# The final norm moved into the last item's branches of an expert loop, on one core

## Chip, cores and metric

One NeuronCore of a Trainium2 chip runs the whole kernel. The metric is the device time in microseconds (us), the median of several runs.

## What is computed

One decoder block on 1024 tokens of width 1024, in fp32: a mixer (short convolution, differential attention, attention into a memory), a feed-forward part in which each token goes to 4 of 32 experts, and a final RMSNorm. The change concerns the last two steps:

```python
x = x + moe_ffn(h, router_w[l], router_b[l], w_gate_up[l], b_gate_up[l], w_down[l], b_down[l])
return rmsnorm(x, final_norm_g)      # y = x * rsqrt(mean(x * x) + eps) * g
```

`moe_ffn` gives each token the sum of its four experts' outputs, each times its gate.

## The kernel before

**Phases.** The mixer and the router run first (about 590 us). They leave in HBM the rows of x (`residual_rows`, `acc_d` in the code), the normed rows for the experts (`h_d`), and for each expert the list of its tokens.

**Items.** The rest is a loop over items. An item is one expert with up to 256 of its rows: one block of 128 rows, a full one and a short one of 64, or two full ones. A table computed on the chip holds each item's expert, list and size. Every engine runs the same loop (groups of 4, inside it `it`) and reads the sizes of this and the next item from the table. `by_size` picks one of three bodies written out one behind the other: `("full",)`, `("full", "short")`, `("full", "full")`. There are 35 items; the last has one block.

**An item's work.** The expert's weights come in 12 units of 1 MB (units 0 to 7 gate and up, 8 to 11 down), each into its slot of `weight_ring`; `home(u)` is the slot of unit u. Each matmul is done in parts: ACT copies a unit to a high half (`high_unit`, L1150), VectorE subtracts for the low half, in place in the ring (`low_unit`, L1564), and TensorE uses both (`use_unit`, L688). It counts `w_used` up per unit, after which SyncE may load the slot anew. Between the units ACT computes the sigmoid of the gate (L1185, L1191), VectorE the product (L1603 to L1622), and TensorE turns the result (L922), which ACT and VectorE split (`a_high` L1198, `a_low` L1585) before the down units. The order on each engine is written out by hand in `item`: on ACT `high_unit` 8 and 9, the next item's x (`x_high`), `high_unit` 10 and 11, `a_high` 1, next item's units, `results`; on VectorE `low_unit` 9, `x_low` 0 of the next item (L1575), `low_unit` 10, `a_low` 1, `low_unit` 11, and so on. Units 10 and 11 on TensorE need `a_low` 1.

**Rows in and out.** GpSimd gathers the rows of an item two items ahead (L603) and adds the results, which ACT writes to `y_rows` (L1211), to `residual_rows` by a scatter that adds (L609). For a missing second block it makes an empty transfer (L651, L660), which is there to move a counter.

**The end.** When the last item's scatter has landed, GpSimd signals `all_added`. SyncE then loads the 8 tiles of 128 rows from `residual_rows` into slots of the ring (L532) and the gain of the final norm, one row spread over 128 partitions (L534, its second transfer). Per tile ACT squares and sums (L1276) and takes the root (L1278), for which it loads another function table than the sigmoid's; VectorE takes the reciprocal (L1690) and multiplies (L1691); SyncE writes the tile out (L537).

Of the kernel before, what the change touches and what calls it, by code (L numbers as in the profile page):

```python
# [67 lines left out]
SHORT = P // 2  # L68
LIST = EXPERTS * S
# [17 lines left out]
def hymba_kernel(nc, a, out):  # L87
    ctx = ExitStack()
    with ctx:
        def sb(name, shape, dt=f32):  # L90
            return ctx.enter_context(nc.sbuf_tensor(name, shape, dt))
# [32 lines left out]

        def final_tile(t):

            return ring[:, t // 2, D * (t % 2):D * (t % 2) + D]
# [70 lines left out]
        def w_low_part(u):  # L198
# [50 lines left out]
        e_rstd = sb("e_rstd", [P, NT])  # L249
        h2T = wk[:, 5, :].rearrange("p (k t) -> p k t", k=KD)  # L250
# [41 lines left out]
            "gain_in", "idx_in", "idx_moved", "idx_kept", "all_added", "pick_made",  # L292
# [13 lines left out]
        s_fout = sem("final_out")  # L306
        s_gf = sem("final_gain_in")
# [104 lines left out]
        def _(sp):  # L412
# [117 lines left out]
            sp.wait_ge(s["all_added"], 1)  # L530
            for t in range(NT):
                sp.dma_start(final_tile(t), acc_d[P * t:P * t + P, :]).then_inc(s_final[t], 16)  # L532
                if t == 0:
                    sp.dma_start(wk[:, 5, :], a["final_norm_g"].partition_broadcast(P)).then_inc(s_gf, 16)  # L534
# [7 lines left out]
        def _(pool):  # L542
# [69 lines left out]

            load_list(slice(0, CAP))
# [20 lines left out]
            with pool.Fori(0, MAX_ITEMS // GROUP) as group:  # L634
                size_group = pool.value_load(table[2:3, bass.ds(group * GROUP + 1, 1)], min_val=0, max_val=CAP + 1)
                with pool.If(size_group > 0):
                    with pool.Fori(0, GROUP) as place_in:
# [4 lines left out]
                        with pool.If(size_now > 0):  # L642
                            with pool.If(size_far > 0):
# [10 lines left out]
                            pool.wait_ge(s["y_made"], it * 2 + 3)  # L654
                            pool.sem_inc(s["pool_waited"], 1)
                            scatter(0)
                            pool.wait_ge(s_scatter[0], it * 16 + 32)
                            pool.sem_inc(s["pool_waited"], 1)
                            by_second(pool, size_now, lambda kind: scatter(1, kind),
                                      lambda: pool.dma_start(nothing[0:1, 1, :], ident[0:1, 0:16]).then_inc(s_scatter[1], 16))  # L660
                            pool.wait_ge(s_scatter[1], it * 16 + 32)
                            pool.sem_inc(s["pool_waited"], 1)
                            with pool.If(size_next > 0):
                                pool.wait_ge(s["idx_kept"], it + 1)
# [15 lines left out]
                            with pool.Else():  # L680
                                pool.sem_inc(s["all_added"], 1)
# [327 lines left out]
        def _(act):  # L1009
# [205 lines left out]

            def item(it, size_next, kinds):
# [56 lines left out]

            for t in range(NT):
                act.wait_ge(s_final[t], 16)
                act.activation(wk[:, 4, :], final_tile(t), ACT.Square, accum_out=e_ssq[:, t:t + 1]).then_inc(s["act_chain"], 1)  # L1276
                act.wait_ge(s["act_chain"], 18 + t + 1)
                act.activation(e_std[:, t:t + 1], e_ssq[:, t:t + 1], ACT.Sqrt, scale=1.0 / D, bias=eps[:, :]).then_inc(s_fsq, 1)  # L1278
# [3 lines left out]
        def _(dve):  # L1282
# [350 lines left out]

            def item(it, size_next, kinds):
# [52 lines left out]
            dve.wait_ge(s_gf, 16)  # L1687
            for t in range(NT):
                dve.wait_ge(s_fsq, t + 1)
                link(dve.reciprocal(e_rstd[:, t:t + 1], e_std[:, t:t + 1]))  # L1690
                dve.scalar_tensor_tensor(out=final_tile(t), in0=final_tile(t), scalar=e_rstd[:, t:t + 1], in1=wk[:, 5, :],  # L1691
                                         op0=ALU.mult, op1=ALU.mult).then_inc(s_fdone, 1)

# [22 lines left out]
```

## Time and profile before

| | us |
|---|---|
| median of 3 runs (lowest, highest) | 2270.81 (2268.62, 2271.24) |
| the profiled execution, reported time | 2271.15 |
| the profiled execution, its span | 2269.5 |
| TensorE busy, share of the span | 2156.5, 95% |
| VectorE busy | 1557.7, 69% |
| ACT busy | 1331.5, 59% |
| GpSimd busy | 340.2, 15% |

The span is from the first to the last event of the execution; the reported time has 1.65 us around it. A share of busy time is a mean over stages with different limits, so a stage is read by itself, with the timelines of its engines side by side. ACT is the scalar engine, DVE VectorE, POOL GpSimd, SP SyncE.

### The profile page before, as it was taken

What the parts mean: (1) busy time and instruction counts of PE and PEld (TensorE: products, weight loads), DVE (VectorE), ACT (ScalarE), POOL (GpSimd) and SP (SyncE); (2) the same over time, 40 slices, a digit from 0 to 9 for tenths busy, and PEclk for the clock granted to TensorE, in tenths of its full rate; (3) what the DMA queues carried; (4) which work ended last, traced back from release to release, by engine and by line L of the source; (5) the groups of instructions that cost most, each with busy time, mean ns of one, the idle gap of its engine ahead of it and who ended that gap; (6) DMA issues with size and microseconds to landing.
All of it is one profiled execution on the core that took longest, in us unless ns stands there. A gap on an engine that the chain in (4) does not pass through costs nothing.

```text
span 2269.5 us, 34559 instructions
## 1 busy us (share of the span) xinstructions
PE 2156.5 (95%) x10770; PEld 1790.6 (79%) x10771; DVE 1557.7 (69%) x1641; ACT 1331.5 (59%) x1524; POOL 340.2 (15%) x306
## 2 busy tenths in 40 slices
PE   7999999895999999999999999999999999999993
PEld 6889767895778888877887878788888878888882
DVE  4411289566577577589758989886677897767764
ACT  5111179443565466577657777775555777556654
POOL 1000000023111022022112121221210122111200
PEclk9999989997999999999999999999999999999997
DMA  5111300434787689599869999996676999677854
GB/s 198 57 56 38 111 1 1 183 106 132 260 292 237 207 294 344 192 365 376 306 206 372 371 368 359 371 343 232 222 234 226 355 373 333 228 232 240 306 162 171
DMA packets 265277, 536.75 MB, mean 237 GB/s; under 512 B 14478, under 2 KB 31144, under 8 KB 265132
## 3 DMA queue, kind: packets, MB, share of 16 engines
q1 hardware_dynamic: 248332, 488.26, 60.3%
q0 software_dynamic: 16896, 47.83, 8.6%
q8 instruction: 32, 0.52, 0.1%
q14 instruction: 17, 0.14, 0.0%
HBM read 499.29 MB, written 36.75 MB: 236 GB/s over the span
## 4 chain that ended last, share of the span: by engine, by line
PE 83%; issue 6%; DVE 5%; ACT 3%; DMA 1%; POOL 0%; DVEq 0%; SPq 0%; ACTq 0%; POOLq 0%
PE ps L688 79%; PE ps L915 1%; ACT hT_hi L1150 1%; PE ps L922 1%; DVE hT_lo L1575 1%; DVE w_lo L1564 1%; PE ps L825 1%; ACT region_mem L1185 0%; DVE work L1615 0%; DVE hT_lo L1585 0%; DMA weight_ring<-in_w_mix_in 0%; ACT hT_lo L1198 0%; DVE weight_ring L1691 0%; DVE work L1393 0%; DVE m_max L1355 0%
## 5 line engine op out<-in xcount | busy, mean ns | idle before, releaser
L688 PE MATMUL ps<-hT_hi,hT_lo 128*128 128x512 f32 (+1 forms) x4304 | 1396.4, 388 | 13.2 <-DVE hT_lo L1585 12.3
L688 PEld LDWEIGHTS ps<-hT_hi,hT_lo 128*128 128x128 f32 x4304 | 806.7, 188 | 182.4 <-DVE w_lo L1564 18.2
L1150 ACT ACTIVATE hT_hi<-weight_ring 128x2048 fp32r<-128x2048 f32 x417 | 786.1, 1914 | 174.8 <-PE ps L688 118.4
L1564 DVE TENSOR_TENSOR slots_between<-weight_ring,hT_hi 128x2048 fp32r<-128x2048 f32 x245 | 552.5, 2286 | 129.5 <-ACT hT_hi L1150 128.9
L688 PE MATMUL ps<-slots_between,hT_lo 128*128 128x512 f32 x1344 | 525.7, 391 | 0.0
L1564 DVE TENSOR_TENSOR w_lo<-weight_ring,hT_hi 128x2048 fp32r<-128x2048 f32 x140 | 319.8, 2285 | 33.6 <-ACT hT_hi L1150 33.6
L688 PE MATMUL ps<-w_lo,hT_lo 128*128 128x512 f32 (+1 forms) x896 | 336.0, 375 | 0.0
L688 PEld LDWEIGHTS ps<-slots_between,hT_lo 128*128 128x128 f32 x1344 | 253.4, 189 | 53.9
L688 PEld LDWEIGHTS ps<-w_lo,hT_lo 128*128 128x128 f32 x896 | 168.7, 188 | 30.3
L609 POOL DMA_INDIRECT residual_rows<-work,idx_now x48 | 121.8, 2537 | 469.5 <-ACT work L1211 274.9
L603 POOL DMA_INDIRECT work<-normed_rows,idx_far x49 | 86.2, 1759 | 442.1 <-PE ps L915 269.8
L688 PE MATMUL ps<-mem_there,picked 128*128 128x512 f32 x288 | 123.5, 429 | 8.8 <-issue 5.9
L1585 DVE TENSOR_TENSOR hT_lo<-ps,hT_lo 128x512 fp32r<-128x512 f32 x96 | 58.9, 636 | 99.1 <-ACT hT_lo L1198 99.1
L1185 ACT ACTIVATE region_mem<-ps,limits 128x512 f32<-128x512 f32 x78 | 52.3, 681 | 123.1 <-PE ps L688 122.6
L688 PE MATMUL ps<-hT_hi,w_hi 128*128 128x512 f32 x256 | 101.1, 395 | 7.5 <-DVE hT_lo L1309 7.5
L589 POOL DMA_INDIRECT expert_lists<-pay,dest_i x32 | 32.6, 1020 | 497.2 <-DVE dest_i L1494 489.9
L1592 DVE TENSOR_TENSOR work<-ps,work 64x512 f32<-64x512 f32 x54 | 36.8, 682 | 101.1 <-ACT work L1169 54.4
L688 PE MATMUL ps<-hT_lo,w_hi 128*128 128x512 f32 x256 | 100.4, 392 | 0.0
L688 PE MATMUL ps<-hT_hi,w_lo 128*128 128x512 f32 x256 | 100.4, 392 | 0.0
L1334 DVE COPY weight_ring<-ps 128x512 f32<-128x512 f32 x18 | 12.4, 691 | 124.5 <-PE ps L688 124.5
L1160 ACT ACTIVATE hT_lo<-ps 128x512 fp32r<-128x512 f32 (+1 forms) x96 | 48.3, 556 | 69.2 <-PE ps L915 69.2
L688 PE MATMUL ps<-last_slot,hT_lo 128*128 128x512 f32 (+1 forms) x256 | 87.2, 364 | 0.0
(251 smaller groups left out, 2418.6 us busy)
## 6 DMA issues: line engine op xcount, KB each, us to landing
weight_ring<-in_w_gate_up SPq DMA_DIRECT2D x280, 1024.0 KB, 7.8
weight_ring<-in_w_down SPq DMA_DIRECT2D x140, 1024.0 KB, 6.3
weight_ring<-in_w_mix_in SPq DMA_DIRECT2D x10, 1024.0 KB, 5.8
weight_ring<-in_x SPq DMA_DIRECT2D x8, 512.0 KB, 8.1
weight_ring<-in_w_mix_out SPq DMA_DIRECT2D x4, 1024.0 KB, 5.3
work<-in_x SPq DMA_DIRECT2D x8, 512.0 KB, 4.6
residual_rows<-work SPq DMA_DIRECT2D x8, 512.0 KB, 3.3
normed_rows<-work SPq DMA_DIRECT2D x8, 512.0 KB, 3.6
```

The lines of the kernel that those rows point to most:

```text
L589: pool.indirect_dma_start(list_d[:, :], bass.IndirectOffsetOnAxis(ap=dest_i[:, i, c:c + 1], axis=0), pay[:, i, c, :], None).then_inc(s["li ...
L603: pool.indirect_dma_start(xg[rows, b, :], None, h_d[:, :], bass.IndirectOffsetOnAxis(ap=idx_far.bitcast(i32)[rows, b, 0:1], axis=0)).then_ ...
L609: pool.indirect_dma_start(acc_d[:, :], bass.IndirectOffsetOnAxis(ap=idx_now.bitcast(i32)[rows, b, 0:1], axis=0), y_rows[rows, b, :], None, ...
L688: return pe.matmul(o, l, r, start=first, stop=last)
L825: last = pe.transpose(ps[:, 4 + b // 4, P * (b % 4):P * (b % 4) + P], wk[:, 2 * (n % 2), P * b:P * b + P], ident[:, :])
L915: last = pe.transpose(ps[:, bank + half, P * k:P * k + P], xg[:, b, HALF * half + P * k:HALF * half + P * k + P], ident[:, :])
L1150: act.activation(w_high_part(u), ring[:, home(u), :], ACT.Copy).then_inc(s["w_high_made"], 1)
L1160: ins = act.activation(x_split[:, 4 * half:4 * half + 4, b, 0, cols], ps[:, bank + half, :].rearrange("p (k t) -> p k t", t=P)[:, :, cols] ...
L1185: ins = act.activation(sig_b[rows, b, :], gate_b[rows, b, :] if kind == "short" else ps[:, out_bank("g", c, b, kinds), :], ACT.Relu, scale ...
L1564: dve.tensor_tensor(w_low_part(u), ring[:, home(u), :], w_high_part(u).bitcast(f32), ALU.subtract)\
L1585: ins = dve.tensor_tensor(low_place(a_split[:, ks, b], kind), ps[:, turn_bank(c, b), :].rearrange("p (k t) -> p k t", t=P)[:, :, cols], a_ ...
L1592: dve.tensor_tensor(place, ps[0:SHORT, bank, :], place, ALU.add).then_inc(s["sum_made"], 1)
```

## The change

The stage behind the loops is gone. Its work goes into the branches that an engine takes in the last item (`size_next` is 0):

- GpSimd, on entering the last item, signals `earlier_added`. It gathers the item's own rows of `residual_rows` into SBUF, and at the end, when these rows are finished (`rows_made`) and all 8 tiles are written out (`s_fout`), scatters them into `out`, without adding. The adding scatter and the empty transfer of the last item are gone.
- SyncE, in the last item, waits for `earlier_added`, loads the 8 tiles into the slots of units 0 to 3 as these are used, and behind them the gain into the slot of unit 4. Its loop checks the size of this item rather than the next, so that it gets there.
- ACT: `final_squares` for tiles 0 to 3 where `x_high` 0 of the next item would stand, for tiles 4 to 7 where the next item's units would stand; each waits for the gain first, takes one root over four tiles and ends with a load of the sigmoid's table. Behind `results` it squares the item's own rows (`rows_std_of`).
- VectorE: `final_norms` for four tiles at the answering places, and `rows_finished` for the item's own rows.

The diff, cut to its core (a line "..." marks what is left out):

```diff
         def final_tile(t):
 
-            return ring[:, t // 2, D * (t % 2):D * (t % 2) + D]
+            return ring[:, home(t // 2), D * (t % 2):D * (t % 2) + D]
...
 (SyncE)
-                size_group = sp.value_load(table[2:3, bass.ds(group * GROUP + 2, 1)], min_val=0, max_val=CAP + 1)
+                size_group = sp.value_load(table[2:3, bass.ds(group * GROUP + 1, 1)], min_val=0, max_val=CAP + 1)
...
+                        with sp.Else():
+                            now = sp.value_load(table[2:3, bass.ds(k + 1, 1)], min_val=0, max_val=CAP + 1)
+                            with sp.If(now > 0):
+                                sp.wait_ge(s["earlier_added"], 1)
+                                for t in range(NT):
+                                    sp.wait_ge(s["w_used"], k * 12 + (HI_SLOTS + t // 2 + 1))
+                                    sp.dma_start(final_tile(t), acc_d[P * t:P * t + P, :]).then_inc(s_final[t], 16)
+                                sp.wait_ge(s["w_used"], k * 12 + (HI_SLOTS + FINAL_GAIN_UNIT + 1))
+                                sp.dma_start(final_gain(), a["final_norm_g"].partition_broadcast(P)).then_inc(s_gf, 16)
...
 (GpSimd, last item)
-                                pool.sem_inc(s["all_added"], 1)
+                                pool.sem_inc(s["earlier_added"], 1)
+                                for b in range(BLOCKS):
+                                    pool.wait_ge(s_xturned[b], it + 1)
+                                pool.sem_inc(s["pool_waited"], 1)
+                                rows_gather(0)
...
+                                pool.wait_ge(s["rows_made"], 1)
+                                pool.wait_ge(s_fout, 16 * NT)
+                                pool.sem_inc(s["pool_waited"], 1)
+                                rows_scatter(0)
...
 (ACT)
+            def final_squares(n, tiles):
+                act.wait_ge(s_gf, 16)
+                for t in tiles:
+                    act.wait_ge(s_final[t], 16)
+                    act.wait_ge(s["act_chain"], 18 + t)
+                    act.activation(final_junk(), final_tile(t), ACT.Square, accum_out=e_ssq[:, t:t + 1]).then_inc(s["act_chain"], 1)
+                act.wait_ge(s["act_chain"], 18 + tiles[-1] + 1)
+                cols = slice(tiles[0], tiles[-1] + 1)
+                act.activation(e_std[:, cols], e_ssq[:, cols], ACT.Sqrt, scale=1.0 / D, bias=eps[:, :]).then_inc(s_fsq, 1)
+                act.preload_act_table(ACT.Sigmoid)
+
+            def rows_std_of(kinds):
+                act.preload_act_table(ACT.Sqrt)
+                act.wait_ge(s["act_chain"], 18 + NT)
+                for b, kind in enumerate(kinds):
+                    act.wait_ge(s["rows_summed"], b + 1)
...
+                act.preload_act_table(ACT.Sigmoid)
...
                 with act.If(size_next > 0):
                     x_high(0, it + 1, "full")
+                with act.Else():
+                    final_squares(0, FINAL_EARLY)
                 high_unit(it, 10)
                 high_unit(it, 11)
                 a_high(it, 1, kinds)
...
+                with act.Else():
+                    final_squares(1, FINAL_LATE)
                 for c in range(2):
                     results(it, c, kinds)
...
+                with act.If(size_next < 1):
+                    rows_std_of(kinds)
...
 (VectorE)
+            def final_norms(n, tiles):
+                dve.wait_ge(s_fsq, n + 1)
+                cols = slice(tiles[0], tiles[-1] + 1)
+                dve.reciprocal(e_rstd[:, cols], e_std[:, cols]).then_inc(s["final_rstd"], 1)
+                dve.wait_ge(s["final_rstd"], n + 1)
+                for t in tiles:
+                    dve.scalar_tensor_tensor(out=final_tile(t), in0=final_tile(t), scalar=e_rstd[:, t:t + 1], in1=final_gain(),
+                                             op0=ALU.mult, op1=ALU.mult).then_inc(s_fdone, 1)
+
+            def rows_finished(it, kinds):
+                dve.wait_ge(s["y_made"], it * 2 + 3)
...
                 with dve.Else():
                     dve.sem_inc(s_xlow[0], 1)
+                    final_norms(0, FINAL_EARLY)
                 low_unit(it, 10)
                 a_low(it, 1, kinds)
...
+                with dve.If(size_next < 1):
+                    final_norms(1, FINAL_LATE)
+                    rows_finished(it, kinds)
```

## Rows read from the trace of the kernel before

**Rows 1.** Waits: engine, line, waited for: us in total, times, longest.

```profile
POOL nothing L660 <- DMA residual_rows<-work,idx_now: 162.8, 22, 8.7
```

**Rows 2.** Windows, one-block item: PE, PEld, DVE, ACT, POOL busy, PEclk, DMA share, GB/s.

```profile
1254.50:1291.70 37.20, 36.39 (x168) 29.71 (x167) 32.85 (x23) 28.31 (x23) 7.67 (x8) 1.00 1.05 375
```

**Rows 3.** Timeline, same item, VectorE and TensorE: start, us, [idle before <-releaser].

```profile
1280.72 2.29 DVE L1564 TENSOR_TENSOR w_lo<-weight_ring,hT_hi 128x2048 fp32r<-128x2048 f32 x1
...
1283.75 0.47 PE L688 MATMUL ps<-hT_hi,hT_lo 128*128 128x512 f32 x1 [0.81 <-DVE hT_lo L1585]
```

**Rows 4.** Chain of waits that ended last, the tail: start, us, what.

```profile
2235.84 6.12 DMA residual_rows<-work,idx_now
...
2242.75 1.56 DMA nothing<-ident
...
2244.62 0.36 SPq L532
...
2245.49 6.10 DMA weight_ring<-residual_rows
...
2251.62 1.16 ACT work L1276 x2
```

**Rows 5.** Timeline, last item and tail, ACT.

```profile
2217.21 7.32 ACT L1150 ACTIVATE hT_hi<-weight_ring 128x2048 fp32r<-128x2048 f32 x4
...
2234.36 0.69 ACT L1211 ACTIVATE work<-ps,idx_now 128x512 f32<-128x512 f32 x1 [1.89 <-PE ps L688]
2247.86 1.06 ACT L1276 ACTIVATE work<-weight_ring 128x1024 f32<-128x1024 f32 x1 [12.81 <-DMA weight_ring<-residual_rows]
...
2249.02 1.28 ACT L1278 ACT_TABLE_LOAD   x1
2250.32 0.30 ACT L1278 ACTIVATE e_std<-e_ssq,eps 128x1 f32<-128x1 f32 x1
```

**Rows 6.** Timeline, the items before the last, GpSimd.

```profile
2142.07 0.76 POOL L598 DMA_DIRECT2D idx_far<-expert_lists  x1 [1.36 <-issue]
...
2215.32 0.19 POOL L666 COPY idx_now<-idx_next 128x4 f32<-128x4 f32 x1 [5.00 <-DMA residual_rows<-work,idx_now]
```

**Rows 7.** Timeline, TensorE: after an idle stretch early on; unit 9 of the last item.

```profile
418.93 1.12 PE L849 MATMUL ps<-ident,region_v 128*128 128x128 f32 x4 [4.60 <-DVE region_v L1433]
...
2225.62 0.50 PE L688 MATMUL ps<-mem_there,picked 128*128 128x512 f32 x1 [0.45 <-DVE w_lo L1564]
```

**Rows 8.** SyncE's timeline; DMA issues 2235 to 2270: count, KB, us to landing.

```profile
2245.49 4.08 SPq L532 DMA_DIRECT2D weight_ring<-residual_rows  x7
...
out_rows<-weight_ring SPq DMA_DIRECT2D x8, 512.0 KB, 6.7
work<-in_final_norm_g SPq DMA_DIRECT2D x1, 512.0 KB, 5.3
```

**Rows 9.** Windows in the tail, columns as in rows 2.

```profile
2247.50:2248.50 1.00, 0.00 (x0) 0.00 (x0) 0.00 (x0) 0.64 (x1) 0.00 (x0) 0.50 0.67 242
...
2251.50:2252.50 1.00, 0.00 (x0) 0.00 (x0) 0.71 (x1) 0.88 (x1) 0.00 (x0) 0.50 1.02 418
```

**Rows 10.** Timeline, tail, VectorE.

```profile
2253.33 1.28 DVE L1691 SCALAR_TENSOR_TENSOR weight_ring<-weight_ring,e_rstd,work 128x1024 f32<-128x1024 f32 x1
```

**Rows 11.** Windows around idle stretches of TensorE, for the granted clock (PEclk).

```profile
423.00:424.00 1.00, 1.00 (x10) 1.00 (x9) 1.00 (x5) 0.00 (x0) 0.00 (x0) 0.86 1.05 387
...
2238.00:2240.00 2.00, 0.00 (x0) 0.00 (x0) 0.00 (x0) 0.00 (x0) 0.00 (x0) 0.79 0.90 125
```

**Rows 12.** All gathers of L603: from issue to landing.

```profile
DMA to landing us min/median/max: 4.1/7.1/9.1
```

**Rows 13.** Timeline, ACT at the start of two one-block items.

```profile
1254.53 5.53 ACT L1150 ACTIVATE hT_hi<-weight_ring 128x2048 fp32r<-128x2048 f32 x3 [1.56 <-issue]
...
2200.24 5.62 ACT L1150 ACTIVATE hT_hi<-weight_ring 128x2048 fp32r<-128x2048 f32 x3 [0.72 <-issue]
```

**Rows 14.** DMA queues between 400 and 650 us: packets, MB, share.

```profile
q8 instruction: 15, 0.25, 0.4%
```

More of the change, by code:

```diff
@@ L68 @@
 SHORT = P // 2
+FINAL_GAIN_UNIT = 4
+FINAL_EARLY, FINAL_LATE = range(0, 4), range(4, S // P)
 LIST = EXPERTS * S
@@ L306, in hymba_kernel @@
         s_fout = sem("final_out")
+        s_rows_in = [sem(f"rows_in{b}") for b in range(BLOCKS)]
+        s_rows_out = [sem(f"rows_out{b}") for b in range(BLOCKS)]
         s_gf = sem("final_gain_in")
@@ L611, in scatter, with rows_gather, rows_scatter @@
                     y_rows[rows, b, :], None, compute_op=ALU.add).then_inc(s_scatter[b], 16)
+            def rows_gather(b, kind="full"):
+                rows = rows_of(kind)
+                pool.indirect_dma_start(
+                    xg[rows, b, :], None, acc_d[:, :],
+                    bass.IndirectOffsetOnAxis(ap=idx_now.bitcast(i32)[rows, b, 0:1], axis=0)).then_inc(s_rows_in[b], 16)
+            def rows_scatter(b, kind="full"):
+                rows = rows_of(kind)
+                pool.indirect_dma_start(
+                    out[0, :, :], bass.IndirectOffsetOnAxis(ap=idx_now.bitcast(i32)[rows, b, 0:1], axis=0),
+                    y_rows[rows, b, :], None, bounds_check=S - 1, oob_is_err=False).then_inc(s_rows_out[b], 16)
             load_list(slice(0, CAP))
@@ L652, in _ @@
                                 pool.sem_inc(s["pool_waited"], 1)
[L654 to L662, printed above, removed]
-                            with pool.If(size_next > 0):
+                            with pool.If(size_next > 0):
+                                pool.wait_ge(s["y_made"], it * 2 + 3)
+                                pool.sem_inc(s["pool_waited"], 1)
+                                scatter(0)
+                                pool.wait_ge(s_scatter[0], it * 16 + 32)
+                                pool.sem_inc(s["pool_waited"], 1)
+                                by_second(pool, size_now, lambda kind: scatter(1, kind),
+                                          lambda: pool.dma_start(nothing[0:1, 1, :], ident[0:1, 0:16]).then_inc(s_scatter[1], 16))
+                                pool.wait_ge(s_scatter[1], it * 16 + 32)
+                                pool.sem_inc(s["pool_waited"], 1)
                                 pool.wait_ge(s["idx_kept"], it + 1)
@@ L1214, in results @@
                 ins.then_inc(s["rest_made"] if "short" in kinds else s["y_made"], 1)
+            def final_squares(n, tiles):
[13 more added lines that the diff above has]
+                    act.wait_ge(s["rows_summed"], b + 1)
+                    rows = rows_of(kind)
+                    act.activation(final_junk()[rows, :], xg[rows, b, :], ACT.Square, accum_out=rows_ssq[rows, b:b + 1])\
+                        .then_inc(s["rows_squared"], 1)
+                    act.wait_ge(s["rows_squared"], b + 1)
+                    act.activation(rows_std[rows, b:b + 1], rows_ssq[rows, b:b + 1], ACT.Sqrt, scale=1.0 / D, bias=eps[rows, :])\
+                        .then_inc(s["rows_std"], 1)
+                act.preload_act_table(ACT.Sigmoid)
             def item(it, size_next, kinds):
@@ L1272, in _ @@
                             act.sem_inc(s["act_item"], 1)
[L1274 to L1278, printed above, removed]
         @block.vector
@@ L1632, in results @@
                     dve.tensor_scalar(place, place, idx_now[0:SHORT, b, 1:2], None, ALU.mult).then_inc(s["y_made"], 1)
+            def final_norms(n, tiles):
[8 more added lines that the diff above has]
+                dve.wait_ge(s["y_made"], it * 2 + 3)
+                for b, kind in enumerate(kinds):
+                    rows = rows_of(kind)
+                    dve.wait_ge(s_rows_in[b], 16)
+                    dve.tensor_tensor(xg[rows, b, :], y_rows[rows, b, :], xg[rows, b, :], ALU.add).then_inc(s["rows_summed"], 1)
+                for b, kind in enumerate(kinds):
+                    rows = rows_of(kind)
+                    dve.wait_ge(s["rows_std"], b + 1)
+                    dve.wait_ge(s["rows_summed"], b + 1)
+                    dve.reciprocal(rows_rstd[rows, b:b + 1], rows_std[rows, b:b + 1]).then_inc(s["rows_rstd"], 1)
+                    dve.wait_ge(s["rows_rstd"], b + 1)
+                    ins = dve.scalar_tensor_tensor(out=y_rows[rows, b, :], in0=xg[rows, b, :], scalar=rows_rstd[rows, b:b + 1],
+                                                   in1=final_gain()[rows, :], op0=ALU.mult, op1=ALU.mult)
+                ins.then_inc(s["rows_made"], 1)
             def item(it, size_next, kinds):
@@ L1685, in _ @@
                             dve.sem_inc(s["dve_item"], 1)
[L1687 to L1692, printed above, removed]
 _INS = ["x", "mem", "rel_bias", "attn_norm_g", "w_mix_in", "conv_w", "lambda_qk", "diff_subln_g", "mem_norm_g",
```

22 lines of the change are left out of this document (16 added, 6 removed).

## Prediction

> **What bounds the kernel now.** The page's first part, busy time by engine, names TensorE, and the loop over the items is its loop. Most items have one block of 128 rows: 22 of 35 make the empty transfer that stands for a missing second block [rows 1]. In such an item, 37.20 us long, TensorE works 36.39 us [rows 2] and loses 0.81 us once, waiting for the split of the activations on VectorE [rows 3]. The change leaves TensorE's program alone, so what it can win is in the tail; the chain of waits and the timelines of the last 40 us are the views to read, engine by engine.
>
> The tail of now: the last result leaves ACT at 2235.05 (2234.36 + 0.69) [rows 5]. GpSimd starts the adding scatter at 2235.84 and it lands 6.12 us later; an empty transfer takes 1.56 us more; the first tile is asked for at 2244.62 and the last write ends the span at 2269.5 [rows 4]. That is 34.5 us behind the last result. The DMA engines are the limit of its second half: 8 tiles in, the gain, 8 tiles out, 8.9 MB at about 420 GB/s, with a slow stretch at 242 GB/s where the gain is broadcast [rows 9]. The change wants to do the 8 tiles while TensorE still works, and leave only the last item's own rows for the end.
>
> **The change part by part.** The sum follows the last item in the clock of the profiled execution (span 2269.5, reported 2271.15, so 1.65 around it; the median of the three runs is 2270.81, 0.34 below the profiled one).
>
> *When the loads can start.* GpSimd says that the earlier items are added when it enters the last item. Its last act in the item before is the copy that ends at 2215.51 [rows 6]. Then it waits for its own signal and reads the table three times. Elsewhere such a wait, one read and the making of a transfer cost 1.36 us of idle time together [rows 6]. So three reads cost between 0.5 and 3.2 us; I take 2.3, and the first tile is asked for at 2217.8. The slots are long free by then: TensorE is past units 0 to 4, which are used in order ahead of unit 9, and that one begins at 2225.62 [rows 7].
>
> *When the gain lands.* SyncE asks for 8 tiles, 0.58 us each [rows 8], and for the gain last. The queue delivers in the order asked: now the first tile lands 3.24 us after its request (2244.62 to 2247.86) [rows 4, 5], the gain, asked second, takes 5.3 us [rows 8], and ACT gets the second tile, asked for at 2245.49, 6.10 us later [rows 4]. In the changed kernel 4.19 MB of tiles and GpSimd's gather of the last item's rows (0.52 MB) go ahead of it. These 4.71 MB take 11.2 us at 420 GB/s, the gain 2.2 us at 242 GB/s [rows 9], and 2.0 us go to start and completion (the first tile's 3.24 less the 1.2 that its 0.52 MB take): 15.4 us, so the gain is there at 2233.2.
>
> *What waits for it.* This is the heart of it. The first act of `final_squares` is a wait for the gain, and on ACT this stands ahead of `high_unit` 10, 11 and `a_high` 1. Without the gain ACT would get there at 2220.9, two of its four weight copies after 2217.21 [rows 5]; it now stands until 2233.2, and TensorE's units 10 and 11 wait behind it. TensorE is done with unit 9 at about 2228.5 and then idles for 19 us.
>
> *ACT from 2233.2:* four squares with their sums, 1.16 each [rows 4] and a signal between, 4.9; table load 1.28; root 0.30 [rows 5]; signal to VectorE at 2239.7. Table of the gate, 1.28: 2241.0. Weight copies 10 and 11, 1.83 each (7.32 / 4), and `a_high`, 0.6: 2245.3. Then the late four tiles: squares to 2250.2, load and root to 2251.8, table of the gate to 2253.1.
>
> *VectorE from 2239.7:* reciprocal and four products at 1.28 (1.2 apart) [rows 10]: 2244.8. The low half of weight 10 at 2.29 (2.2 apart) [rows 3]: 2247.1; the split of the activations, 0.69: 2247.7; low half 11: 2249.9.
>
> *TensorE:* unit 10 begins at 2247.85. When it stopped at 2234.3 in the kernel before, its clock was down to half in the stretch 2238 to 2240 (granted 0.79 of full) and it came back only 4.3 us after work began at 418.93 (0.86 in 423 to 424) [rows 7, 11]. So I charge the first 4.4 us at half clock: 10 matmuls at 0.45 us, the other 14 of the two units at 0.23 (36.39 us for 168 of them, transposes among them, are 0.22 each [rows 2]): 2255.6. ACT's second result is done at 2256.3, which is 21 us later than now.
>
> *The tail behind that:* VectorE finishes the late four products (from 2251.9) at 2256.9 and adds the gathered rows (1.2): 2258.2. Square and sum on ACT 1.25, root 0.30, reciprocal 0.2, product 1.28: 2261.4. From ACT's result to the start of a scatter GpSimd took 0.79 us [rows 4, 5]: 2262.2. A scatter without adding isn't in the trace: gathers of the same size land in 4.1 us at best [rows 12], the adding scatter of the undisturbed tail in 6.12 [rows 4]; I take 5.0, nearer to the quiet gather, whose traffic is the same: 2267.2. The eighth tile's write, asked for at 2257.0, lands in at most 6.7 us [rows 8], 2263.7, so its wait comes at worst 1.5 us later than the rows are ready, and at best is hidden. GpSimd then goes through the loop once more, three reads: 1.5 us. End at 2268.9.
>
> So the sum is 0.6 us under the span of now: 34.5 us of tail become 12.6, and 21 of the 22 us are paid back as a hole in the middle of the last item. As a reported time 2270.5 for the profiled execution, 2270.2 for the median.
>
> *What every item pays.* ACT skips two new blocks and one at the end, VectorE one longer block and one at the end. ACT's gap between items is 0.72 us where it falls through to the end of the loop body, and 1.56 where it jumps over the two other bodies [rows 13], so a jump costs between 0 and 0.84. ACT has cover, for it is busy 28.31 of an item's 37.20 us [rows 2] and waits for TensorE in the rest. VectorE's next low half follows with no idle time where a jump stands today [rows 3]. I take nothing. If the cover is gone, the delay adds to TensorE's 0.81.
>
> A rule that speaks against the change is on the Trainium skill's page "Runtime: NRT & Kernel Launch", section "Instruction fetch mechanics": a taken branch to code outside a small window forces a fetch by DMA and stalls. In this trace the queues of instructions carry packets up to 650 us [rows 14] and have no row between 660 and 2200 us, where the loop runs more than 30 times; so today the bodies fit. No run shown has the longer ones.
>
> The page "ScalarE: Activation LUTs" of the Trainium skill, section "What ACT_TABLE_LOAD costs", adds a drain of about 1.38 us to every switch. The trace disagrees: the square begins at 2247.86, the load 1.16 us later, which is what a square with its sum takes [rows 4], and the root begins 0.02 us after the load's end [rows 5]. By the page's figure the three switches on the path would make the sum 4.1 us longer.
>
> **The rivals.** *The gain comes early.* If its packets don't queue behind the tiles, it lands 5.3 us after its request at 2222.4, at 2227.7, 5.5 us earlier, and all behind it moves along: 2264.7. For it: the transfers use 16 engines, and order between them isn't proven. Against: the landings of now come in the order asked.
>
> *The jumps are uncovered.* In each of 22 items VectorE's jump over the longer block, between the split of x and the low half of weight 10, delays the split of the activations for which TensorE already waits [rows 3]. At 0.84 each that is 18 us: 2288. It decides from 0.2 us an item. For it: there is no slack behind. Against: a jump stands there already and shows nothing.
>
> *The loop outgrows its instruction buffer.* ACT's three bodies grow by half. Each item would then fetch code on ACT; the price of a small transfer is at least the 1.56 us of the empty one [rows 4], twice an item, once to leave a body and once to come back: 3.1 us in each of 34 items, 106 us with nothing covered, half of it if ACT's idle time takes the other half: 2323 to 2376, so about 2340. For it: nothing in the trace shows how much the buffer holds. Against: today three bodies run without a fetch. It is the rule of the page on the runtime.
>
> *Switches of the table with a drain:* 2274.3, still no change that can be measured.
>
> **How the numbers follow.** Forecast as summed: 0.68. Gain early: 0.12. Jumps: 0.10. Fetches: 0.06. Drains: 0.04. The forecast's unknowns are the start of the loads (-1.8 to +0.9), the gather (it may not compete: -1.2), the scatter (-0.9 to +1.1), GpSimd's last round and the write's wait (-1 to +1.5), and small gaps between some 25 steps (up to +2): 2265.5 to 2277. The range goes down to 2263.5 to take in the early gain, and leaves out the jumps and the fetches (0.16). What this kernel's measurement can tell from no change is 0.2%, 4.5 us. Under 2266.3: the early gain and a twentieth of the rest, 0.17. Over 2275.3: jumps, fetches and a twentieth, 0.21. Within: 0.62.
>
> **What would show it.** A hole of 15 to 20 us on TensorE in the last item, ended by VectorE's split, with the clock at half behind it; ACT waiting for the gain's transfer for about 12 us, longest of all its waits; the second result of the last item near 2256 and not 2235; six table loads on ACT in the last item, none in others; a one-block item still 37.2 us long. If ACT's wait for the gain is under 5 us, the forecast is too slow; if a one-block item is over 37.4 us, the jumps or fetches decide; if loads start after 2220, all is later by as much.

## The result, and the profile after

| | before | changed |
|---|---|---|
| median, us | 2270.55 (4 runs) | 2574.62 (4 runs, 2573.85 to 2576.03) |
| ratio | | 1.134 (1.132 to 1.136) |
| span of the profiled execution, us | 2269.5 | 2572.2 |
| TensorE busy, us (share) | 2156.5 (95%) | 2218.9 (86%) |

The change costs 304 us, 13%. The tail, on which nearly all of the prediction was spent, can't hold that much: what was 2269.5 us long had 34.5 us behind the last result. So the first look goes to one stretch in the middle. Windows of the changed kernel, columns as in [rows 2]:

```profile
1400.00:1800.00 400.00, 326.63 (x1412) 263.10 (x1413) 261.51 (x190) 224.75 (x192) 78.37 (x54) 0.91 0.79 264
```

and the same stretch before:

```profile
1400.00:1800.00 400.00, 396.58 (x1831) 326.74 (x1830) 306.47 (x252) 262.44 (x245) 75.14 (x57) 1.00 0.84 284
```

In 400 us TensorE does 1412 matmuls where it did 1831. No engine does more than before, bar GpSimd by 3 us, and the DMA engines move 264 GB/s rather than 284; everything waits. Of what TensorE loses, 70 us are idle time. Another 21 come of slower matmuls, 0.231 us each rather than 0.217, with the clock granted at 0.91 on average rather than 1.00. The waits of the changed kernel (engine, line, waited for: us in total, times, longest) name it:

```profile
ACT hT_hi L1197 <- issue: 327.5, 31, 16.8
DVE slots_between L1635 <- ACT hT_hi L1197: 325.2, 40, 16.2
...
PE ps L735 <- DVE slots_between L1635: 224.7, 34, 12.0
...
DVE slots_between L1635 <- issue: 155.4, 13, 14.5
```

"issue" is time in which an engine waits for nothing that the profile shows. Before, the first copy of an item on ACT had 56.3 us of it in all, 2.4 at most. The timelines of one item show where it stands (compare ACT's 1.56 us in [rows 13]):

```profile
1416.80 5.51 ACT L1197 ACTIVATE hT_hi<-weight_ring 128x2048 fp32r<-128x2048 f32 x3 [10.32 <-issue]
...
1421.95 6.70 DVE L1635 TENSOR_TENSOR slots_between<-weight_ring,hT_hi 128x2048 fp32r<-128x2048 f32 x3 [13.23 <-issue]
```

The DMA queues of the changed kernel between 700 and 2200 us (packets, MB, share) say what that is:

```profile
q14 instruction: 271, 2.22, 0.4%
```

These are packets of 8192 bytes on a queue of instructions, some ten an item. Before, this queue has no row in that stretch. So the reading to be tested is that ACT and VectorE fetch their own code anew in every item.

### The profile page after: what moved, and what is told of

Same layout as the page of the kernel before. It is cut to its first block, busy times and chain, and to the rows that moved or that the text cites. A ratio compares the mean times of both kernels' runs of the same rounds, so it can differ in the third digit from the quotient of the medians.

```text
span 2572.2 us, 34729 instructions
## 1 busy us (share of the span) xinstructions
PE 2218.9 (86%) x10770; PEld 1823.9 (71%) x10771; DVE 1557.7 (61%) x1638; ACT 1335.8 (52%) x1526; POOL 365.5 (14%) x308
## 4 chain that ended last, share of the span: by engine, by line
PE 55%; issue 24%; DVE 11%; ACT 4%; DVEq 2%; DMA 1%; ACTq 1%; POOL 0%; SPq 0%; POOLq 0%
PE ps L735 52%; DVE slots_between L1635 6%; ACT hT_hi L1197 2%; PE ps L969 1%; PE ps L962 1%; DVE hT_lo L1646 1%; DVE w_lo L1635 1%; PE ps L872 1%; DVEq L1782 1%; DVEq L1781 1%; ACT region_mem L1232 0%; DVE work L1686 0%; DMA weight_ring<-in_final_norm_g 0%; ACT hT_lo L1245 0%; DVE hT_lo L1656 0%
## 5 line engine op out<-in xcount | busy, mean ns | idle before, releaser
L735 PE MATMUL ps<-hT_hi,hT_lo 128*128 128x512 f32 (+1 forms) x4304 | 1440.4, 398 | 257.3 <-DVE slots_between L1635 224.7
L735 PEld LDWEIGHTS ps<-hT_hi,hT_lo 128*128 128x128 f32 x4304 | 830.3, 194 | 449.0 <-DVE slots_between L1635 239.1
L735 PE MATMUL ps<-slots_between,hT_lo 128*128 128x512 f32 x1344 | 543.7, 405 | 0.0
L735 PEld LDWEIGHTS ps<-slots_between,hT_lo 128*128 128x128 f32 x1344 | 264.9, 197 | 56.7
L630 POOL DMA_INDIRECT residual_rows<-work,idx_now x47 | 110.8, 2357 | 468.9 <-ACT work L1258 270.4
L624 POOL DMA_INDIRECT work<-normed_rows,idx_far x49 | 69.6, 1420 | 644.1 <-PE ps L962 537.1
L735 PEld LDWEIGHTS ps<-mem_there,picked 128*128 128x128 f32 x288 | 55.3, 192 | 36.2 <-issue 13.8
```

What stands on the lines that cost most here:

```text
L624: pool.indirect_dma_start(xg[rows, b, :], None, h_d[:, :], bass.IndirectOffsetOnAxis(ap=idx_far.bitcast(i32)[rows, b, 0:1], axis=0)).then_ ...
L630: pool.indirect_dma_start(acc_d[:, :], bass.IndirectOffsetOnAxis(ap=idx_now.bitcast(i32)[rows, b, 0:1], axis=0), y_rows[rows, b, :], None, ...
L735: return pe.matmul(o, l, r, start=first, stop=last)
```

## Experiments

A loop's length below is its count of instructions in the compiled code (64 bytes each, so 128 to a packet), and its place the number of its first one in the engine's code. Before, the outer loop is 247 long on ACT and 230 on VectorE; changed, 370 and 286. The inner loop, `it`, begins 6 later and ends 2 earlier.

**Is it the length alone?** The kernel before, with a branch that no item takes behind the bodies:

```diff
                             by_size(act, size_now, lambda kinds: item(it, size_next, kinds))
+                            with act.If(size_now < 1):
+                                for _ in range(122):
+                                    act.sem_inc(s["act_item"], 1)
```

and the same with 55 on VectorE. This gives the lengths of the changed kernel without a line of its work. First on both engines, then on ACT alone, then on VectorE alone.

> The kernel before, with instructions that never run (a branch never taken) put behind the three bodies of an item, so many that the loops of ACT and VectorE are as long as in the changed kernel: 370 instructions instead of 247 on ACT, 286 instead of 230 on VectorE. Nothing of the final stage is moved. Theory 'the loop outgrows its instruction buffer': the queue of instructions moves packets in every item, ACT and VectorE idle by 5 to 13 us between items, and the time is near the changed kernel's, 2500 to 2600 us. Rival 'the work in the branches or its waits cost it': within 5 us of 2270.

> The same with ACT's loop alone lengthened to 370 instructions, VectorE's left at 230. If ACT's fetches carry the loss: 2450 or more, half of the packets of instructions of the kernel with both. If VectorE's carry it: under 2330.

> The same with VectorE's loop alone lengthened to 286 instructions, ACT's left at 247. If 286 instructions still fit the buffer of VectorE, no packets beyond 650 us and 2270; if not, VectorE's fetches come in every item, and the time lies between 2400 and 2570, since VectorE has less idle time than ACT.

Measured: 2598.52 (ratio 1.144, 1.142 to 1.146), 2583.22 (1.137) and 2547.39 (1.122). Code that is never run costs all that the change costs, and 24 us more; why the changed kernel pays less than this one isn't shown. It isn't a sum: +275 on VectorE and +311 on ACT make +327 together. In the changed kernel both engines stall in the same stretch of an item (the timelines above), which would explain it. The queue of instructions over the whole run, both, ACT alone:

```profile
q14 instruction: 368, 3.01, 0.4%
```

```profile
q14 instruction: 191, 1.56, 0.2%
```

**The moved work with short loops.** Two bodies in place of three, in the changed kernel and in the one before (an item with a short second block is computed as two full ones, in both):

```diff
-                with eng.If(size < P + SHORT + 2):
-                    body(("full", "short"))
-                with eng.Else():
-                    body(("full", "full"))
+                body(("full", "full"))
...
```

> The changed kernel with two bodies in place of three: items with a short second block run the body for two full ones, so the loops are short (233 instructions on ACT, 174 on VectorE). The nine items concerned cost TensorE about 12 us more each, some 110 us in all. Theory of fetches: no packets of instructions in the loop, 2340 to 2420 us, and one-block items back at 37.2 us. Rival 'the jumps over the longer blocks cost': one-block items at 37.5 to 38 us. The tail as summed in the prediction: TensorE idles 19 us in the last item, ACT waits 12 us for the gain, and the end comes 13 us behind ACT's last result.

> The kernel before with two bodies, as in the changed kernel with two bodies (2373.8 us); against it, it shows what the moved stage costs without any fetch. By the forecast's sum with its last term put right (GpSimd's own end takes about 12 us behind its last landing, not 1.5): the moved stage is about 9 us slower, so this one takes 2363 to 2367 us. By the sum as it stood: 2374. Were the jumps to cost something in each item: under 2355.

2373.81 (1.045, 1.044 to 1.047) against 2365.08 (1.042, 1.040 to 1.043): with loops of 233 and 174 the moved stage costs 8.7 us, not 304, and the queue of instructions is back at 17 packets. A one-block item is untouched: in the same 400 us this kernel does as many matmuls as the kernel before. The windows of the changed kernel with two bodies:

```profile
1400.00:1800.00 400.00, 396.80 (x1831) 327.04 (x1830) 266.13 (x201) 228.64 (x206) 58.76 (x50) 1.00 0.77 257
```

**Where is the limit?** VectorE's loop in the kernel before, at 254 and at 270 (23 and 39 increments in the branch):

> The kernel before with VectorE's loop lengthened by instructions that never run, to 246 in the inner loop and 254 in the outer. If the buffer holds 256 in a row: 2270 and no packets of instructions behind 650 us. If it holds whole blocks of 128 at fixed places, three of which VectorE's loop touches already: also 2270.

> The same at 262 and 270 instructions. If the buffer holds 256 in a row: packets in the loop and over 2450. If it holds three whole blocks of 128, and the loop reaches no fourth one: 2270.

2271.69 (1.000, 0.999 to 1.001) and 2538.67 (1.118). Sixteen instructions make 267 us, so it is a step and not a slope, and a limit of 256 by length seemed settled. It wasn't. ACT at 270:

> The kernel before with a branch that no item takes behind the bodies of the item loop on ACT alone, so that ACT's outer loop has 270 instructions rather than 247 (the inner one 262 rather than 239); VectorE stays at 230. Theory (ACT and VectorE hold the same 256 instructions in a row, and what does not fit costs a pass of fetches in each item): about what a longer loop cost on ACT, 2540 to 2585, with over 150 packets of instructions. Rival one (ACT holds more than VectorE): 2270 to 2274. Rival two (the cost grows with the instructions beyond the limit, of which 14 here and 114 in the longer one): 2290 to 2330.

2269.76 (1.000, 0.999 to 1.001): nothing, where 270 on VectorE had cost 267 us. Either each engine has its own limit, or the place of a loop in the code counts. For the second: let the code be cut into blocks of 128 instructions, the first of which begins some instructions ahead of the code's first one (the offset). The loops that had cost nothing would then touch three blocks, and the others four, if that offset is 61 to 73. This can be put to the test without a change of any length, by increments of an unused semaphore as the engine's very first instructions:

```diff
+            for _ in range(20):
+                dve.sem_inc(s["nowhere"], 1)
             dve.wait_ge(s["vecT_ps"], 1)
```

> The kernel before with VectorE's loop lengthened to 270 instructions, which alone cost 267 us, and with 20 increments of an unused semaphore ahead of all of VectorE's work, so that the loop begins at instruction 842 of its code rather than 822. Theory (three blocks of 128 instructions fit, four don't; by the runs so far the blocks begin 61 to 73 instructions ahead of the code's first one): 842 to 1111 touches three blocks, so 2269 to 2274 and 17 packets of instructions or so. Rival (the limit is one of length, on VectorE between 254 and 270): 2535 to 2545, as unmoved.

> The kernel before with ACT's loop lengthened to 370 instructions, which alone cost 311 us, and with 82 increments of an unused semaphore ahead of all of ACT's work: the loop begins at instruction 701 rather than 619. Theory of blocks: its inner part, 707 to 1068, touches three blocks by the same offset of 61 to 73, though it is longer than any loop that fitted so far: 2269 to 2278. Rival one (a limit by length between 270 and 370 on ACT): about 2583, as unmoved. Rival two (blocks, but with another offset on ACT than on VectorE): either value, and the fetches then tell which part is missed.

VectorE's 270, moved from 822 to 842: 2271.66 (1.000, 0.999 to 1.001). Twenty more instructions took all of the 267 us back. ACT's 370, moved from 619 to 701: 2377.11 (1.046), down from 2583, but 106 us are left. Its queue of instructions and its windows:

```profile
q14 instruction: 74, 0.61, 0.1%
```

```profile
1400.00:1800.00 400.00, 383.12 (x1755) 313.32 (x1755) 296.09 (x239) 254.76 (x237) 80.62 (x56) 0.99 0.84 279
```

The packets come once in a group of four items, five at a time. With an offset of 61 to 66 that is just what should be: 707 and the offset make 768 or more, a border of blocks, and 701 and the offset less, so the inner loop begins behind the border and the outer one ahead of it. Then 8 instructions more should end the rest. The same two moves on the changed kernel itself, all three bodies; the second run has SyncE ask for the gain ahead of the tiles:

```diff
+                                sp.wait_ge(s["w_used"], k * 12 + (HI_SLOTS + FINAL_GAIN_UNIT + 1))
+                                sp.dma_start(final_gain(), a["final_norm_g"].partition_broadcast(P)).then_inc(s_gf, 16)
                                 sp.wait_ge(s["earlier_added"], 1)
                                 for t in range(NT):
...
-                                sp.wait_ge(s["w_used"], k * 12 + (HI_SLOTS + FINAL_GAIN_UNIT + 1))
-                                sp.dma_start(final_gain(), a["final_norm_g"].partition_broadcast(P)).then_inc(s_gf, 16)
```

> The changed kernel, all three bodies, with the same 82 increments ahead of ACT's work and 20 ahead of VectorE's, nothing else. Theory: no fetches in the items, and what is left is the moved stage: the difference of the two kernels with two bodies, 8.7 us, on top of 2270: 2277 to 2283. Rival (position isn't it): about 2575. If only one of the two engines fits: 2545 to 2585.

> As the changed kernel moved to three blocks, but SyncE asks for the gain ahead of the 8 tiles. Theory: as with two bodies, where this brought 11.6 us: 2265 to 2271, no slower than the kernel before. Rival (the gain helps less with three bodies, or fetches remain): 2274 to 2283, or over 2540.

2368.42 (1.044) and 2359.74 (1.040): both expectations of a whole cure missed, as that of ACT's moved loop did, and for the same reason, with the same 74 packets. The gain ahead of the tiles brings 8.7 us. Now with 90 increments on ACT rather than 82:

> The changed kernel with 90 increments of the unused semaphore ahead of ACT's work (82 before) and 20 ahead of VectorE's. Theory: ACT's outer loop, 709 to 1078, now touches three blocks, as the inner one did; no fetches in the loop at all, 17 packets or so over the run, and only the moved stage is left, 8.7 us by the kernels with two bodies: 2277 to 2283. Rival (long loops pay once a group wherever they lie): about 2368, as with 82.

2282.32 (ratio 1.005, 1.0035 to 1.0063): of the 304 us, 292 are gone, with not one line of the change taken back. The queue of instructions and the windows of this kernel:

```profile
q14 instruction: 21, 0.16, 0.0%
```

```profile
1400.00:1800.00 400.00, 396.55 (x1831) 326.69 (x1830) 307.40 (x251) 261.62 (x244) 77.83 (x57) 1.00 0.84 283
```

1831 matmuls in 400 us, as before; behind 660 us one packet of instructions is left, at 842 us. Blocks of 128 account for the 18 kernels of these experiments, the kernel before and the changed one. VectorE's inner loop of 262, from 828, which fetched in every item, narrows the offset to 63 to 66. The trace of the kernel before shows these borders by itself, in code that runs once: of the eight packets between 73 and 391 us, one comes when ACT has done 63, 190, 318 and 445 instructions, and one when VectorE has done 62, 192, 321 and 448 (by the engines' own records, which no view above lists).

Whether three blocks are what an engine keeps isn't settled. Two lines of 256 instructions would fit every run too, if on ACT such a line began at 702 to 707 of the code and on VectorE at 829 to 833, half a line apart. Against it: the packets come singly, one for each 128 instructions, at the same places on both engines. No run has a loop that touches four blocks and yet only two such lines, which would decide. Which block is given up for a fetched one, and what the engine holds ahead, the runs don't show either.

**What the moved stage is worth.** Three runs change its order. With two bodies: the gain ahead of the tiles, and then also `final_squares(0)` and `final_norms(0)` put with those of the late tiles, behind units 10 and 11:

```diff
                 with act.Else():
-                    final_squares(0, FINAL_EARLY)
...
                 with act.Else():
+                    final_squares(0, FINAL_EARLY)
                     final_squares(1, FINAL_LATE)
```

> The changed kernel with two bodies and the gain asked for ahead of the tiles. If the hole in the last item is the wait for the gain at the end of the queue: ACT's first square waits for the gain and tile 0 only, about 6 us instead of 13, tile 3 lands as the squares run, and the end comes 5 to 8 us earlier: 2366 to 2369 us against 2373.8. If the hole has another cause: no change beyond 2 us.

> The same, and the first four tiles done together with the last four, behind the weight copies 10 and 11 and the last split, so that no work of the final stage stands ahead of what TensorE needs. TensorE's hole of 19 us in the last item goes to under 1 us. ACT's results still wait for eight squares, two roots and four table loads; ACT has everything else done 8 us earlier than with the gain first. If the hole is worth what it lasts: 2358 to 2364 us. If the same work on ACT sets the end anyway: 2364 to 2369.

2362.21 (1.040, 1.038 to 1.041) and 2361.47 (1.039, 1.038 to 1.041), so 11.6 us for the gain's place; the 0.7 for the order is no more than the runs can tell from nothing, and so are the 2.9 and 3.6 us by which the two now stand under the 2365.08 of their own kernel before. I had given the gain 5 to 8: I hadn't counted that the wait for it and TensorE's hole go together. With the gain first the hole is 8.8 us rather than 20.1. Taking the rest of it away helps little, since ACT's squares, which had filled it, then stand behind units 10 and 11. The last kernel is the same on the three bodies, moved to fit:

> As the one before, and the gain asked for ahead of the tiles, and the squares and products of tiles 0 to 3 moved to stand with those of tiles 4 to 7, behind units 10 and 11. Theory: by the kernels with two bodies these two edits bring 12.3 us: 2265 to 2270, 0 to 0.3% under the kernel before. Rival (a jump over long bodies costs something in each item once fetches are gone): 2271 to 2280.

2270.00 (1.000, 0.999 to 1.001), 12.3 us less than with the move alone, as the two edits had brought with two bodies: the cure and the better order together come back to the kernel before, and no further.

**Without the stage in the loop.** SyncE and GpSimd as in the change, with the gain first, but ACT's and VectorE's part behind the loops (lengths 247 and 232). GpSimd gathers the last item's rows in the loop and scatters both blocks of them behind it:

```diff
                 with act.If(size_next > 0):
                     x_high(0, it + 1, "full")
-                with act.Else():
-                    final_squares(0, FINAL_EARLY)
...
+            act.preload_act_table(ACT.Sqrt)
+            act.wait_ge(s_gf, 16)
+            for n, what in enumerate(FINAL_ORDER):
...
+                act.activation(final_junk(), src, ACT.Square, accum_out=ssq_at).then_inc(s["act_chain"], 1)
+                act.wait_ge(s["act_chain"], 18 + n + 1)
+                act.activation(std_at, ssq_at, ACT.Sqrt, scale=1.0 / D, bias=eps[:, :]).then_inc(s_fsq, 1)
```

> A kernel in which SyncE and GpSimd do as in the changed one (loads in the last item, the gain now ahead of the tiles, the item's own rows gathered), but ACT and VectorE do the final stage behind the loops, so that their loops are as long as in the kernel before (247 and 232 instructions), and GpSimd's scatter of the finished rows stands behind its loop too. No hole in the last item and no packets of instructions. Sum: last result at 2235 as before, ten squares and roots at 1.46 on ACT after a load of 1.28, last product 2252.5, last write landed 2255.3, two scatters 2257.5, drain of GpSimd 6.3: 2264, so 4 to 8 us faster than the kernel before, 2263 to 2267 us. If the fetch of the code behind the loops costs as much as in the changed kernel: 2270 or more.

2274.47 (1.0015, 1.0006 to 1.0025): slower, where 4 to 8 us faster had been expected. It isn't fetches, the other reading: no packet of instructions comes behind 636 us. ACT and VectorE have to walk the rounds of the loop that have no item before they come to what stands behind it. Their timelines:

```profile
2239.21 1.28 ACT L1343 ACT_TABLE_LOAD   x1 [5.37 <-issue]
```

```profile
2240.94 2.36 DVE L1795 TENSOR_TENSOR work<-work 128x1024 f32<-128x1024 f32 x2 [11.60 <-issue]
```

ACT's 5.37 us are these rounds. VectorE's 11.60 are, by its own record, 4.5 us of waiting for the last result and 7.0 of rounds. Then GpSimd scatters, waits for the landing and ends 6.3 us behind it. The last version takes the item's rows last, lets VectorE walk on without waiting for the last result (GpSimd signals that it is there), and has SyncE wait for the last scatter, so that GpSimd's end runs beside it:

```diff
-            for b in range(BLOCKS):
-                pool.wait_ge(s_rows_out[b], 16)
...
             sp.wait_ge(s_fout, 16 * NT)
+            for b in range(BLOCKS):
+                sp.wait_ge(s_rows_out[b], 16)
```

> The kernel with the final stage behind the loops, mended in three places that its profile shows: the item's own rows come behind the eight tiles on ACT and VectorE, so that their work runs while the last writes land; VectorE goes round the empty rounds of its loop before it waits for the last result; SyncE and not GpSimd waits for the last scatter, so that GpSimd's closing drain of 6 us runs beside it. Last write landed at 2256 to 2257, second scatter made at 2260, drain to 2266: 2266 to 2269 us as reported, 2 to 4 us under the kernel before and 6 under the first form.

2269.04 (0.9991, 0.9982 to 1.0000), the lowest ratio of all: 2 us, at the edge of what can be measured. GpSimd's end still closes the run: its last instruction is done at 2262.65 of 2262.9 us, 6.12 behind the making of the second scatter. Only the scatter's landing is hidden.

## Why the prediction was wrong

**The step that failed** is "What every item pays", with its "I take nothing". It weighed the price of a jump over the longer bodies, and that was right: with no fetches 400 us of the loop hold 1831 matmuls, as before. What it missed, 292 us of fetched code, had been written down as a rival, "The loop outgrows its instruction buffer". It was given 0.06, for ACT alone, and priced at 2340; the time was 2574.6, and VectorE's fetches by themselves cost 275 us. The argument against it, "today three bodies run without a fetch", only says that 247 and 230 fit. It says nothing of 370 and 286, and no row of before could. Loops that grow by half on ACT and by a quarter on VectorE, the two engines that feed TensorE, with no row for what fits, deserved far more.

**The price of the rival** was too low by a factor of three. I took two stalls of 1.56 us an item, the time of the smallest transfer, 3.1 in all. From the changed kernel to the same one moved into three blocks it is 2574.6 - 2282.3 = 292 us over 34 items, 8.6 us each. With one engine's loop lengthened, an item has five packets in a row, most of them 3 to 5 us from one to the next. An item takes one path through the code and so I counted its two jumps. The five packets look like block after block of a whole round of the loop; why five and not four, the runs don't show. The 292 us also hold the slower matmuls seen in the first windows.

The Trainium skill's page "Runtime: NRT & Kernel Launch", section "Instruction fetch mechanics", was the rule that spoke against the change, and was right in kind. Its sizes are 32 KiB for these engines, 512 instructions, in two lines of 256. The runs show packets of 128 that come singly. A loop of 270 is far under the 512, and still fetched in one place. Two lines of 256 allow that where a loop touches three of them, and fit the other runs if the lines begin as said above. Whether 384 or 512 instructions are held, no run here shows.

**The sum of the last item** can be read from the changed kernel moved to 709, which has no fetches:

| | forecast | measured |
|---|---|---|
| first tile asked for | 2217.8 | 2220.4 |
| ACT's wait for the gain | 12.3 | 13.2 |
| hole on TensorE | 19 | 19.8 |
| last result leaves ACT | 2256.3 | 2259.4 |
| from there to the scatter | 5.9 | 5.3 |
| scatter, to its landing | 5.0 | 3.5 |
| from there to the end | 1.7 | 13.0 |
| end of the span | 2268.9 | 2281.2 |

Its waits and timelines, in the views of [rows 1], [rows 5], [rows 6] and [rows 8]:

```profile
PE ps L735 <- DVE hT_lo L1660: 19.8, 1, 19.8
...
ACT weight_ring L1270 <- DMA weight_ring<-in_final_norm_g: 13.2, 1, 13.2
```

```profile
2220.42 4.09 SPq L552 DMA_DIRECT2D weight_ring<-residual_rows  x8
2224.63 0.42 SPq L554 DMA_DIRECT2D weight_ring<-in_final_norm_g  x1
...
2235.71 1.06 ACT L1270 ACTIVATE weight_ring<-weight_ring 128x1024 f32<-128x1024 f32 x1 [13.24 <-DMA weight_ring<-in_final_norm_g]
...
2258.68 0.69 ACT L1260 ACTIVATE work<-ps,idx_now 128x512 f32<-128x512 f32 x1 [2.10 <-PE ps L735]
...
2264.68 1.02 POOL L642 DMA_INDIRECT out_rows<-work,idx_now  x1 [40.21 <-DVE work L1730]
```

- *The gain lands behind the tiles*: right. It took 11.1 us from its request there, and 5.0 where it is asked for first (the rival "The gain comes early" falls).
- *The clock*: right in kind, and a little too short. TensorE begins unit 10 at 2250.26 with its clock granted at 0.50, and the clock's record has it there until 2255.96, 5.7 us and not 4.4; a matmul takes 0.43 us from one to the next at first and 0.22 to 0.23 at the end. A window of the first 4.4 us:

```profile
2250.30:2254.70 4.40, 4.40 (x11) 3.43 (x12) 2.58 (x3) 4.26 (x7) 0.00 (x0) 0.50 0.00 0
```

- *No drain at a switch of the table*: right. Load and root follow with no gap in the moved stage too, where the Trainium skill's page "ScalarE: Activation LUTs" ("What ACT_TABLE_LOAD costs") would have 1.38 us more for each:

```profile
2240.60 1.28 ACT L1273 ACT_TABLE_LOAD   x1
2241.89 0.30 ACT L1273 ACTIVATE e_std<-e_ssq,eps 128x4 f32<-128x4 f32 x1
```

- *"GpSimd then goes through the loop once more, three reads: 1.5 us"*: wrong, and the one large miss of the sum. The loop has 48 rounds in 12 groups for 35 items. When the landing is seen at 2268.2, GpSimd still walks one round and three empty groups, 1.23 us each, until 2274.9. Then one instruction at the end of its program takes 6.12 us (from 2274.88 in GpSimd's own record, as are these times; the views above don't list them). Before, the same two steps ran from 2244.7 to 2256.4 beside the traffic of the tiles, where they cost nothing. The change takes that cover away. A step that other work hides has to be priced as it would be without that work.

With that one term right the sum would have been 11.3 us longer, 2281.5 as a reported time, against 2282.3 measured. That it comes so near is in part luck: the last result was 3.1 us later than summed, and the two steps to the landing 2.1 us shorter. So even without the fetches the forecast "no change that can be measured" was wrong: 0.49% (0.35 to 0.63) slower.

**The cause**, then: 292 of 304 us are fetches of code on ACT and VectorE, shown by code that never runs and by a move of 90 and 20 instructions that takes them away. The other 11 to 12 are the moved stage: it pays back the tail of now by a hole of 19.8 us and by GpSimd's end, which nothing hides any more. Edits of the order show the first of these; the second is read from the records, and no run took it away alone. What an engine keeps of its code, and by which rule, is open as said above.

## What to carry to other kernels

Count the instructions of every loop an engine runs before adding to a branch of it, also to one that is taken once: what is never executed counts as much as what is. A loop that has outgrown what its engine keeps shows as idle time with no releaser at the same place in each round, together with packets on the queue of instructions in mid-loop; the test is to put dead code into the old kernel, and the cure is less code in the loop or another place for it. And when a tail is shortened, follow each engine to the end of its own program, not only the data.

## What the hardware showed that I had not expected

- The place of a loop decides, not its length alone: ACT ran 370 instructions with no fetch when they began at 709, VectorE 270 at 842; VectorE's 270 at 822 cost 267 us. By the blocks of 128, up to 257 instructions can't touch four wherever they begin, and between that and 384 it is a matter of place; the longest loop that ran free here had 370. So an edit far ahead of a loop, in code that runs once, can make a kernel 12% slower or faster.
- TensorE's loop of 1705 instructions ran with no fetches at all: its packets, 16384 bytes each, end by 641 us in every run.
- Two engines that fetch in the same stretch cost hardly more than one: 327 us against 311 and 275.
- The last instruction of GpSimd's program took 6.0 to 6.3 us in 19 of 20 profiles; in the last version, where it began before the second scatter was made, it ended 6.12 us behind that.
- The scatter at the end lands in 3.3 us where it doesn't add, and in 6.12 where it does [rows 4]. But it also moves less, 0.32 MB against 0.52, and no run sets the two apart.
